# Attention on TensorE: values, then all turns in a row, over three PSUM banks

## The reference

```python
def _attend(q, k, v):
    s = jnp.einsum('bqkgd,bskd->bkgqs', q, k).astype(jnp.float32) * ATTN_SCALE
    p = jax.nn.softmax(s, axis=-1).astype(v.dtype)
    return jnp.einsum('bkgqs,bskd->bqkgd', p, v)
...
    # layer 0 and 1: 1024 latent rows attend to 256 context + 1024 latent rows
    o_lat = lax.map(lambda qb: _attend(qb, k_all, v_all), q_blocks)
    # layer 0 only: 256 context rows attend to the context
    if with_ctx_out:
        o_ctx = _attend(heads_q(bq_c), k_ctx, v_ctx).reshape(B_, Lc, B_WIDTH)
...
    mod_lat = silu_c @ w_ada[l] + b_ada[l]     # shifts, scales and gates
```

## Time and profile before

| what | us |
|---|---|
| three timed executions | 3931.43, 3925.73, 3928.97 (median 3928.97) |
| span of the profiled execution, first to last instruction | 3925.8 |
| PE busy over the span | 3733.4 (95%) |
| DVE / ACT busy over the span | 2061.4 / 1423.8 |
| layer 0 attention, first scores to the next stage's first matmul | 386.28 to 691.12 |
| layer 1 attention, the same | 1297.57 to 1582.19 |

### The profile page before, as it was taken

How to read it: one execution, slowest core, us unless ns; L and a number is a source line. 1 busy time by engine, 2 the same in 40 slices (tenths; PEclk the granted TensorE clock), 3 DMA queues, 4 the chain that set the end, 5 groups by cost and what they waited for, 6 DMA issues and landing times.

```text
span 3925.8 us, 49593 instructions
## 1 busy us (share of the span) xinstructions
PE 3733.4 (95%) x17744; PEld 2421.2 (62%) x17744; DVE 2061.4 (53%) x4105; ACT 1423.8 (36%) x3493; POOL 1052.7 (27%) x1132
## 2 busy tenths in 40 slices
PE   7999999999999999999999999999999999979995
PEld 4887566655788666655466666785566688433331
DVE  4876667345588666345275464442233344354445
ACT  3434556123233555224344443421233322221113
POOL 2255000032226000032043344542212264013331
PEclk9999999999999999999999999999999999989998
DMA  5001210022101232122101001101101110149997
GB/s 208 28 1 65 108 55 22 30 81 76 67 28 44 86 129 77 42 84 76 55 6 41 22 27 70 44 22 56 45 12 43 69 44 29 63 190 362 376 355 296
DMA packets 88767, 346.95 MB, mean 88 GB/s; under 512 B 21176, under 2 KB 53440, under 8 KB 69712
## 3 DMA queue, kind: packets, MB, share of 16 engines
q1 hardware_dynamic: 70096, 304.94, 20.9%
q0 software_dynamic: 18432, 38.85, 2.6%
HBM read 401.31 MB, written 37.83 MB: 112 GB/s over the span
## 4 chain that ended last, share of the span: by engine, by line
PE 84%; DVE 8%; issue 3%; ACT 3%; DMA 1%; PEldq 0%; POOL 0%; DVEq 0%; SPq 0%; PEld 0%; POOLq 0%; ACTq 0%
PE psum L88 18%; PE psum L345 17%; PE psum L94 9%; PE psum L2184 6%; PE psum L4147 5%; PE psum L2640 5%; PE psum L1509 4%; PE psum L1480 4%; PE psum L4169 3%; PE psum L2890 3%; PE psum L2658 1%; PE psum L503 1%; PE psum L2847 1%; PE psum L2021 1%; PE psum L2571 0%
## 5 line engine op out<-in xcount | busy, mean ns | idle before, releaser
L345 PE MATMUL psum<-arena 128*128 128x256 f32 x3920 | 862.9, 381 | 23.0 <-ACT arena L358 8.3
L345 PEld LDWEIGHTS psum<-arena 128*128 128x128 f32 x3920 | 741.7, 191 | 134.1 <-issue 18.9
L88 PE MATMUL psum<-arena 128*128 128x512 f32 (+3 forms) x2176 | 765.9, 506 | 6.6 <-DVEq L221 5.7
L88 PEld LDWEIGHTS psum<-arena 128*128 128x128 f32 x2176 | 408.6, 191 | 303.2 <-issue 252.0
L94 PEld LDWEIGHTS psum<-arena 128*128 128x128 f32 (+2 forms) x3020 | 342.7, 142 | 220.3 <-issue 144.9
L94 PE MATMUL psum<-arena 128*128 128x128 f32 (+2 forms) x3020 | 440.5, 280 | 28.6 <-DMA arena<-hn_scratch,arena 5.9
L2640 PE MATMUL psum<-arena 128*128 128x512 f32 (+1 forms) x640 | 285.4, 573 | 9.0 <-DVE arena L2691 4.8
L2184 PE MATMUL psum<-arena 128*128 128x512 f32 x576 | 259.9, 600 | 0.9 <-ACT arena L2308 0.9
L4147 PE MATMUL psum<-arena 128*64 x512 | 227.4, 597 | 6.2 <-issue 4.0
L4148 PE MATMUL psum<-arena 128*64 128x512 f32 x512 | 227.4, 597 | 0.0
L216 DVE SCALAR_TENSOR_TENSOR arena<-arena 128x256 f32<-128x256 f32 (+1 forms) x164 | 126.7, 778 | 145.6 <-ACT arena L213 145.1
(11 more groups left out here) (432 smaller groups left out, 5818.9 us busy)
## 6 DMA issues: line engine op xcount, KB each, us to landing
arena<-w_gu SPq DMA_DIRECT2D x32, 2048.0 KB
arena<-w_ada SPq DMA_DIRECT2D x24, 2048.0 KB
arena<-w_dn SPq DMA_DIRECT2D x32, 1024.0 KB
arena<-w_in SPq DMA_DIRECT2D x12, 2048.0 KB
arena<-w_out SPq DMA_DIRECT2D x6, 2048.0 KB
arena<-gate_rows_scratch SPq DMA_DIRECT2D x36, 256.0 KB, 3.4
x_scratch<-arena SPq DMA_DIRECT2D x18, 512.0 KB, 2.8
arena<-x SPq DMA_DIRECT2D x16, 512.0 KB, 9.7
```

The costliest lines, as they stand in the source:

```text
L88: ins = e.matmul(out, l, r, start=(i == 0), stop=(i == n - 1))
L345: ins = e.matmul(P[f.banks[b]][:, 0:c], left[:, k, :], right[:, k, :], start=(k == 0 and i in (1, 4, 5, 6)), stop=(k == 3), skip_group_che ...
```

## The change

The step is written anew on all three engines. PE now does the scores of unit u, all five value groups of u-2 in a row, then all five turns of u-1 in a row, and at the end the turn of the values of u-2 (before: u-3, one step later). A modulation group's matmuls come between values and turns, and its transposes at the end of the same step. All of these take banks 5, 6 and 7 in turn as a ring: `att_ring` lists the users in PE's order, and the n-th waits until the user three places ahead of it has been read. DVE copies turns 0, 1 and 3, ACT 2 and 4 (for short units DVE copies the one turn). ACT copies the values between its two exponentials, and copies turns after both. Short units use two sets of score banks in turn, so that their scores wait for the exponentials of unit u-2 and not u-1.

```diff
+        P_ON_V = (0, 1, 3)
...
-            return P[3 * r][:, 0:NC_T * 128]
+            return P[3 * r + u % 2][:, 0:NC_T * 128]
...
+            def take(*user):
+                i = ring.index(user)
+                if i >= 3:
+                    e.wait_ge(*ring_read(l, ring[i - 3]))
+                return P[5 + i % 3]
...
+                elif n == T:
+                    e.wait_ge(*aexp.of("att", l, u - 1, 0))
+                elif u >= 2:
+                    e.wait_ge(*aexp.of("att", l, u - 2, 0))
...
+            def turn_values(w):
+                b = take("out", w)
+                e.wait_ge(*acop.of("values", l, w))
...
-            for u in range(len(units) + 3):
+            for u in range(len(units) + 2):
+                v, w, mul = u - 1, u - 2, ada_step(l, u)
                 if u < len(units):
...
+                    scores(u)
...
-                for gs, ws in (((0, 1), (0, 1, 2)), ((2, 3), (3, 4))):
-                    for g in gs:
-                        if g < ng:
-                            turn_P(v, g)
-                    if 0 <= w < len(units):
-                        values(w, ws)
-                if ng > 4:
-                    turn_P(v, 4)
-                if w >= 1:
-                    turn_values(w - 1)
...
+                if 0 <= w < len(units):
+                    values(w)
+                if mul is not None:
+                    pe_ada(e, *ada_later(l)[mul], pad1, take("row", mul))
+                if 0 <= v < len(units):
                     e.wait_ge(*aexp.of("att", l, v, 0))
+                    for g in range(att_tiles(l, v) // 2):
+                        turn_P(v, g)
+                if 0 <= w < len(units):
+                    turn_values(w)
                 if mul is not None:
+                    pe_ada_turn(e, *ada_later(l)[mul], mrow1, take("mod", mul), acop)
```

The ring's list, in the order of PE's work in one step, and ACT's new step:

```diff
+                if 0 <= w < len(units):
+                    order.append(("values", w))
+                if mul is not None:
+                    order.append(("row", mul))
+                if 0 <= v < len(units):
+                    order += [("P", v, g) for g in range(att_tiles(l, v) // 2)]
+                if 0 <= w < len(units):
+                    order.append(("out", w))
+                if mul is not None:
+                    order.append(("mod", mul))
...
+                v, w, mul = u - 1, u - 2, ada_step(l, u)
+                for r in (1, 0):
+                    if u < len(units):
...
                         e.activation(Pm[:, u % 2, r * n:(r + 1) * n], att_scores(l, u, r), ACT.Exp, bias=st[:, 2 + r:3 + r],
                                      scale=0.125, accum_out=st[:, 4 + r:5 + r]).then_inc(*aexp.by("att", l, u, r))
+                    if r and w >= 0:
+                        e.wait_ge(*prod.of("values", l, w))
...
+                if mul is not None:
+                    a_ada_row(e, *ada_later(l)[mul], mrow1, att_bank(l, "row", mul))
+                if 0 <= v < len(units):
+                    for g in range(att_tiles(l, v) // 2):
+                        if g not in P_ON_V:
+                            e.wait_ge(*turned.of("P", l, v, g))
+                            e.activation(PT_of(l, v, g), att_bank(l, "P", v, g), ACT.Copy).then_inc(*acop.by("PT", l, v, g))
```

More of the change, by code:

```diff
@@ L1451, in score_parts, with att_ring @@
             return [(0, 1024, 1280), (1, 256, 768), (0, 0, 512), (1, 768, 1280), (0, 512, 1024), (1, 0, 256)]
-        def pe_att(e, l):
[L1454 to L1462, removed]
-                n = att_tiles(l, u) * 128
[L1464 to L1470, removed]
-                for g in gs:
[L1472 to L1478, removed]
+        def att_ring(l):
+            units, order = att_units(l), []
+            for u in range(len(units) + 2):
+                v, w = u - 1, u - 2
+                mul = ada_step(l, u)
+                if 0 <= w < len(units):
[8 more added lines that the diff above has]
+                    order.append(("mod", mul))
+            return order
@@ new lines, in att_bank, with ring_read @@
+        def att_bank(l, *user):
+            return P[5 + att_ring(l).index(user) % 3]
+        def ring_read(l, user):
+            kind = user[0]
+            if kind == "values":
+                return acop.of("values", l, user[1])
+            if kind == "row":
+                return acop.of("ada", *ada_later(l)[user[1]])
+            if kind == "P":
+                return copied_P(l, *user[1:])
+            if kind == "out":
+                return vmul.of("att", l, user[1])
+            return vmul.of("ada", *ada_later(l)[user[1]])
@@ new lines, in pe_att, with scores, values @@
+        def pe_att(e, l):
+            units, ring = att_units(l), att_ring(l)
+            def take(*user):
[3 more added lines that the diff above has]
+                return P[5 + i % 3]
+            def scores(u):
+                t, h = units[u]
+                n = att_tiles(l, u) * 128
+                if u == 0:
+                    last = len(qk_sets(l)) - 1
+                    e.wait_ge(*bcop.of(("qk", l), last, 11))
+                    e.wait_ge(*bsum.of(("qk", l), last, "u3"))
+                    e.wait_ge(*acop.of("qT", l, NT - 1))
+                    e.wait_ge(*acop.of("kT", l, 2 * k_order(l)[-1] + 1))
+                elif n == T:
+                    e.wait_ge(*aexp.of("att", l, u - 1, 0))
+                elif u >= 2:
+                    e.wait_ge(*aexp.of("att", l, u - 2, 0))
+                for r, a_, b_ in score_parts(l, u):
+                    if (r, a_, n) == (1, 0, T):
+                        e.wait_ge(*prod.of("scores", l, u, 0, T))
+                    ins = e.matmul(att_scores(l, u, r)[:, a_:b_], qT[64 * r:64 * r + 64, h // 2, tile(t)],
+                                   kT[64 * r:64 * r + 64, h // 4, a_:b_], start=True, stop=True)
+                    if (r, b_) in ((0, T), (0, n - 256), (1, 256), (1, T)) or n < T:
+                        ins.then_inc(*prod.by("scores", l, u, r, b_))
+            def values(w):
+                t, h = units[w]
+                b, ng = take("values", w), att_tiles(l, w) // 2
+                for g in range(ng):
+                    e.wait_ge(*copied_P(l, w, g))
@@ L1479, in values @@
                     for j in range(2):
-                        ins = e.matmul(P[7][64 * j:64 * j + 64, 0:256],
+                        ins = e.matmul(b[64 * j:64 * j + 64, 0:256],
                                        KV[:, 2 * g + j, 128 + 64 * (h // 4):192 + 64 * (h // 4)],
-                                       PT_of(l, u, g)[:, 256 * j:256 * j + 256], start=(g == 0), stop=(g == ng - 1))
-                    if g == ng - 1:
-                        ins.then_inc(*prod.by("values", l, u))
@@ L1486, in pe_att @@
[L1486 to L1492, removed]
-            for u in range(len(units) + 3):
-                if u < len(units):
[L1496 to L1512, removed]
@@ new lines, in values, with turn_P @@
+                                       PT_of(l, w, g)[:, 256 * j:256 * j + 256], start=(g == 0), stop=(g == ng - 1))
+                ins.then_inc(*prod.by("values", l, w))
+            def turn_P(v, g):
+                b, n = take("P", v, g), att_tiles(l, v) * 128
+                turn(e, [(b[:, tile(2 * j + r)], Pm[:, v % 2, r * n + (2 * g + j) * 128:r * n + (2 * g + j + 1) * 128])
+                         for j in range(2) for r in range(2)], ident).then_inc(*turned.by("P", l, v, g))
+            def turn_values(w):
+                b = take("out", w)
+                e.wait_ge(*acop.of("values", l, w))
+                turn(e, [(b[:, tile(r)], Of[:, 2 * (w % 2) + r, :]) for r in range(2)], ident).then_inc(*turned.by("values", l, w))
@@ L1562, in v_att @@
                                             ).then_inc(*vsta.by("att", l, u, r))
-                v = u - 1
+                v, w, mul = u - 1, u - 2, ada_step(l, u)
                 if 0 <= v < len(units):
[L1565 to L1572, removed]
+                    for g in P_ON_V:
+                        if g < att_tiles(l, v) // 2:
+                            e.wait_ge(*turned.of("P", l, v, g))
+                            e.tensor_copy(PT_of(l, v, g), att_bank(l, "P", v, g)).then_inc(*vcop.by("PT", l, v, g))
+                if w >= 0:
+                    t, h = units[w]
+                    st = sts[:, w % 6, :]
+                    e.wait_ge(*aexp.of("att", l, w, 0))
                     vo.seq(e, e.reciprocal(st[:, 6:8], st[:, 4:6]))
-                    e.wait_ge(*turned.of("values", l, x))
+                    e.wait_ge(*turned.of("values", l, w))
                     if last:
                         e.wait_ge(*last)
-                    y4 = P[6][:, 0:256].rearrange("p (r k d) -> p r k d", r=2, k=2)
-                    e.tensor_reduce(att2, y4.rearrange("p r k d -> p r d k"), AX, ALU.add).then_inc(*vmul.by("att", l, x))
-                    e.wait_ge(*vmul.of("att", l, x))
```

(23 more changed lines are left out.)

29 lines of the change are left out of this document (5 added, 24 removed).

## The result

The changed kernel takes 3953.13 us (median of 4 runs, 3950.95 to 3955.78), the kernel before 3930.20 beside it (3925.73 to 3931.88): a ratio of 1.0065 with a 95% interval of 1.0053 to 1.0077. Run again in the last experiment it took 3951.92 against 3926.69, 1.0060 (1.0047 to 1.0073). So it is slower by about 24 us, where 28 was forecast and the time 3957.

The account below looks back on a forecast made before the run. PE bound the kernel before; a longer loop through DVE and ACT would bind it after. 29.1 + 0.9 - 0.6 - 2 = 27.4, say 28 us, on 3928.97 gave 3957; range 3938 to 3974, narrower 3942 to 3972.

Parts of the forecast that it names:

- rival 1: At each step's end PE's own work decides, not waits: 25 us less, 3904; chance 5%.
- rival 2: PE's clock falls to 0.50 in the row of transposes; some 2.2 us per full step, 128 more, 4085; chance 4%.
- The loop: Scores, maxima, exponentials around the values' copy, turn 2's copy, values' turn, next scores: 8.27 us a plain step, 0.61 more.
- the short units: Layer 0's short units: between -8 us (all idle time goes) and +6 (longer wait each); -2 taken.
- rival 3: Short units give their full 8 us and the loop is 0.3 shorter: some 4 us more, 3933; chance 6%.
- psum-queue depth-cycling: Skill's rule cited against the change: idling between matmul groups could make PE's clock fall in every step; trace spoke against it.
- The modulation step: Step with a modulation group: its transposes wait for DVE's copy of turn 3, 10.21 us; with a plain step 18.48, 0.86 more.
- The sum over full steps: Steps between two full units at full clock, 29 per layer: 15.5 us more in layer 0, 13.6 in layer 1, together 29.1.
- The edges: Outside those full steps: +0.9 us at layer 0's first full units, -0.3 twice at stage ends, -2 in short units.
- The two steps into full units: Layer 0's first two steps of full units grow by the values' copy (0.26) and by 0.61: +0.9 us.
- Each stage's end: One step fewer at the end of each attention stage saves a piece: -0.3 us, twice.
- Outside attention: What follows attention only shifts; DMA has room, and modulation weights asked for at a slower pace arrive no later.

Follow-up runs that it names:

- the last experiment: The changed kernel run again with nothing altered, beside the kernel before: 3951.92 us against 3926.69, ratio 1.0060.
- the first experiment: Against the changed kernel, ACT makes its copy of turn 2 twice: 3984.53 us (one run).
- the six experiments: Six edits of the changed kernel: turn 2 copied twice, turn 4 twice, turn 2 on DVE, values' copy later, one score-bank set, two turn rows; 3916.46 to 3994.08 us.

## Why the prediction was right

The rival theories of the forecast fall. PE's own work does not decide (rival 1): the first experiment lengthens the step by an ACT copy alone. The clock was 1.00 throughout the full steps (rival 2), though PE waited twice in each and did 22 transposes with no other work between them. The loop is 0.04 shorter than forecast and not 0.3, and the short units gave back less than 8 us (rival 3). The Trainium skill ("TensorE: Matmul & The Clock Gate", section "A second HAM failure mode: psum-queue depth-cycling") tells of a kernel that cycled through PSUM banks and idled between groups of matmuls so often that its clock went back and forth. That did not come true here, with waits of 0.3 us by the profile's PE rows and 0.5 by its weight loads.

- *The loop.* Forecast link by link 2.03, 4.32, 5.66, 5.92, 7.26, 7.91 and 8.27; measured 2.03, 4.32, 5.64, 5.90, 7.20, 7.86 and 8.23. The links forecast a little long are the exponentials: 1.32 and 1.30 instead of 1.34 from start to next copy.
- *The modulation step.* Forecast 10.21, measured 10.32. The transposes wait for DVE's copy of turn 3 as worked out; that copy starts 0.09 later than I had it (617.97). Turn 2 started 0.05 earlier than forecast (616.84), so from there to that copy it took 1.13 us where the sum had 0.99. The 0.14 more is as much as the prediction has elsewhere for a piece of transposes that starts anew, and left out here.
- *The sum over full steps.* Forecast 15.5 and 13.6; measured 15.27 (235.90 to 251.17 us, units 10 to 39 of layer 0) and 14.58 (249.44 to 264.02, units 2 to 31 of layer 1, one step of 10.60 in it): 29.85 against 29.1.
- *The edges.* Here the size was off. The short units gave back 4.63 us (33.76 to 29.13) and not 2, which was a choice between -8 and +6. The two steps into full units grew by 0.15 (16.65 to 16.80) and not 0.9, mainly because the scores of the second full unit, at a granted clock of 0.58 where it was 0.50, took 3.97 us and not 4.57. Each stage's end is 0.6 shorter, not 0.3, and the first two steps of layer 1 are 0.1 shorter. So the two stages together are 24.04 us longer (304.84 to 315.02, and 284.62 to 298.48), where 27.4 was worked out.
- *Outside attention.* "What follows only shifts" came out as a sum, by luck: the net is 0.9 us in this pair of profiles, made of 1.7 more ahead of attention, 7.0 less between the two stages and 6.1 more behind the second. The last experiment shows that such stretches move by some 5 us between runs of one kernel.

One place outside attention looks like the change's and is not shown to be. The next stage's first 32 matmuls took 9.12 and 9.13 us before and take 7.43 and 7.44 in the first profile of the changed kernel, in layers 0 and 1. The granted clock is what differs, 0.81 against 1.00. But in the second profile of the same changed kernel it is 1.00 behind layer 0 and 0.81 behind layer 1. Before, behind layer 0; then the changed kernel behind layer 1, first and second profile:

```profile
691.12:700.24 9.12, 9.12 (x32) 7.21 (x33) 1.47 (x3) 0.46 (x2) 1.41 (x2) 0.81 0.12 31
...
1601.01:1608.45 7.44, 7.44 (x32) 6.11 (x33) 1.47 (x3) 0.46 (x2) 1.41 (x2) 1.00 0.64 194
...
1603.86:1612.99 9.13, 9.13 (x33) 7.15 (x34) 1.47 (x3) 0.46 (x2) 1.41 (x2) 0.81 0.48 158
```

The changed kernel and the six experiments pass such a place 16 times in eight profiles, and 3 of them are at 0.81; the one profile of the kernel before has both at 0.81. Each is worth 1.7 us. Whether the new end of the stage makes the full clock likelier stays open.

The mechanism was forecast right, and of the 27.4 us worked out 24.04 were measured in the attention stages; what was missed lies mainly in the edges. The forecast time was 3957 and the measured median 3953.13, in the range of 3938 to 3974 and in the narrower one of 3942 to 3972.

## What to carry to other kernels

Fewer changes of work on a full engine pay only while no loop through the other engines is longer: write the loop down with start times from one step of the trace (here scores, maxima, exponentials, copy, turn, scores) and compare it with the full engine's own work. A ring of buffers ties each user to the reader three places ahead, so look at which engine does that read and what stands before it in that engine's order; the late reader set the step here, and one digit in a tuple moved 0.36 us a plain step. A ring of another size was not tried.

## What was not expected of the hardware

- A second identical ACT copy of 128x512 from PSUM, waiting for the first to land, started 0.63 to 0.65 us after it (606.51 to 607.16), where a copy that waits for nothing of ACT's starts 0.47 after the one before (606.04 to 606.51): waiting for its own result cost ACT some 0.17 us.
- The granted clock at the start of the next stage (1.00 in some places, 0.81 on average in others, where it fell to 0.50 for some 3.4 us and rose again) does not follow from what PE did just before. In both profiles of the changed kernel PE's last pieces of layer 1's attention follow one another at the same distances to 0.01 us (2.31, 2.88, 2.96 and 1.54 us up to the 32 matmuls), and the clock behind them is 1.00 in one and 0.81 in the other.
